# Narrow gate products, state-row spreading and weight splits reordered in a two-layer hybrid decoder step

## The chip, the cores and the metric

One core of a Trainium2 chip runs the whole program. The metric is the device time of one execution in microseconds (us); the median of several runs counts. The engines are TensorE (PE, matrix products), VectorE (DVE, "vector"), ScalarE (ACT), GpSimd (POOL) and SyncE (SP), which issues most loads. Each has its own instruction stream; they wait for one another on semaphores.

## The reference

A prompt of 512 tokens and 8 sample tokens (520 columns in all) go through two layers with shared weights. Layer 0 has gated DeltaNet heads and SSD heads behind one input projection, an output projection `w_out`, and a SwiGLU FFN; layer 1 has latent attention and a second FFN. What the change touches, cut down:

```python
proj = rms_norm(x, norm_g) @ w_in
g_qkv, g_z, g_a, g_b, s_z, s_xbc, s_dt = split(proj)
beta = sigmoid(g_b);  g = -exp(A_log) * softplus(g_a + dt_bias)
dt = softplus(s_dt + ssm_dt_bias)
# recurrences in chunks; at the end of a chunk (for a sample: of its one token)
S = S * exp(last) + einsum('bhjd,bhjv->bhdv', k * exp(last - cum), v_new)
h = h * exp(last) + einsum('bjhn,bjhp->bhpn', B * exp(last - cum), xdt)
x = x + concat([o, y]) @ w_out
x = x + (silu(gate) * up) @ w_down       # gate, up = rms_norm(x) @ w_gate_up
```

The 16 gate columns are g_a (4), s_dt (8) and g_b (4). For the samples each of the 8 sequences has its own states: S of 4 heads x 128 x 128, h of 128 x 512, 2 MB each for all eight. They are decayed, updated by an outer product of a key column and a value row, and stored.

## The kernel before

Activations lie with features on the 128 partitions and 520 tokens in the free dimension, in two halves of 260. Every large weight tile of 128 output features x 1024 is loaded by SP into one of four slots `wring`, rounded to a high half on ACT (`high`, L1191) and completed by a low half on DVE (`low`, L1635). `piece` (L553) then makes 48 products per tile: high weight by high and by low activation, low weight by high activation, over 8 slices of 128 and two halves. A tile goes to bank pair 0/1 or 2/3 of PSUM, alternately, and `gemm_ready` and `tile_taken` hand it over and back. PE's queue runs the stages in the order of `STAGES` (L50): `proj` (7 turns of 4 tiles), the chunked recurrences, `outa` (8 tiles), `gu0` (44), `dn0`, and then layer 1 with `inc`, `uq`, attention, `outc`, `gu1`, `dn1`.

**The gates.** After turn 0 of `proj` PE waits for the scaled gate weights (`gprep_ready`) and for the norm's root, and makes 5 x 8 float32 products in L612 to L617: 128 tokens of `xres` as the stationary operand, `wgate` with 16 columns as the moving one; five more products turn the root into a column. DVE finishes the convolution of turn 0 (`conv_turn`, L1710), then computes softplus and sigmoid from bank 6 (L1735 to L1766), with exponentials from ACT (L1294 to L1298), then goes into the loop of turns 1 to 4 (L1768). A step of that loop evicts a tile (L1720), splits a weight (`low`) and convolves it (L1725 to L1730). ACT applies SiLU and splits weights in the same order (L1272).

**The end of layer 0's mixer.** After the chunks the sample states wait for their update. POOL loads h0, issues the stores of the prompt's states (`rec_stored`), decays s0 and h0 one sequence after the other (L492 to L495), issues two stores of convolution rows and only then adds squares for the next norm (`sum_squares(1)`, L498). PE turns the value rows into rows 0 to 7 (L848 to L855), and ACT copies them to `vrow` and `xrow` (L1411 to L1414). During `outa`, after tile k, `spread_rows(k)` (L857) makes two float32 products per sequence b that copy row b to all 128 partitions, in banks 6 and 7:

```python
mm(PS[:, 6, :], ident[0:8, b:b + 1].broadcast_to([8, 128]), vrow[0:8, :])
```

DVE's `update(b)` (L1988) multiplies bank 6 by the key column (L1992), adds that to s0 once it is decayed (L1995), and does the same for h0 from bank 7 (L1999, L2002). `UPDATES` (L57) puts sequences 6 and 7 behind tile 6. PE waits for update b - 1 before it spreads row b. In `residual` (L1607) DVE waits for `rec_stored`, and then, for each tile k, adds it to `xres`, splits the low half of weight k + 2, makes the low half of the normed activation k - 1 (`gained_low`, L1601), and calls the updates. ACT's `ffn` (L1198) has the same steps: high half of weight k + 2, high half of the activation, its square (L1174), which from the third on waits until POOL has added the one before last. At k = 7 ACT waits for all updates, issues the stores of s0 and h0 (L1208, L1210), and splits the first two weights of `gu0`; their low halves are DVE's, before it takes tile 7. The split weights lie where `vrow`, `xrow` and the update's scratch `supd` lay. After `gu0`'s first tile PE sums the squares over the partitions (`norm_sum`, L599, banks 4 and 5), and ACT makes the root. ACT and DVE then wait until both state stores have landed, since the FFN's activations lie over the states.

## Time and profile before

| | |
|---|---|
| median of 3 runs | 1562.09 us (1559.18 to 1562.7) |
| the profiled execution, its own time | 1566.82 us |
| its span | 1565.1 us |
| mean granted clock of TensorE | 0.971 |
| busy: PE, DVE, ACT, POOL | 96%, 48%, 38%, 10% |

A busy PE is not a PE at its peak: the granted clock says which of its two levels it ran at (1.0 is 2.4 GHz, 0.5 is 1.2 GHz). Idle time of another engine costs nothing as long as PE has work. In the rows below, times are microseconds from the start of the span; a row of a timeline has start, duration, engine, line, operation, output and inputs, and a count where rows are merged; in brackets stands how long the engine was idle before it and what released it. The products have the line of the helper `mm`, L543, so they are told apart by their tiles. `arena` is the large buffer that holds most tensors, s0, h0, `hid`, `mix`, `vrow` and `supd` among them.

### The profile page before, as it was taken

How to read it: one execution, taken by the hardware profiler on the slowest of the kernel's cores; microseconds unless marked ns; L12 is line 12 of the kernel's file. 1: busy time of each engine (PE TensorE's matmuls, PEld its weight loads, DVE VectorE, ACT ScalarE, POOL GpSimd, SP SyncE). 2: the span in 40 equal slices, each digit the busy share in tenths (PEclk: the TensorE clock that was granted, in tenths of full speed). 3: DMA queues.
4: the chain of work that ended last, by engine and by line, in shares of the span. 5: the costliest groups of instructions: out<-in, count | busy, mean ns of one | idle time of the engine just before them, and what ended most of it. 6: DMA issues, size and time to landing. Idle time of an engine off the chain costs nothing.

```text
span 1565.1 us, 29154 instructions
## 1 busy us (share of the span) xinstructions
PE 1504.4 (96%) x11822; PEld 1400.9 (90%) x11822; DVE 753.3 (48%) x1277; ACT 593.6 (38%) x905; POOL 161.0 (10%) x194
## 2 busy tenths in 40 slices
PE   7999988889899999999999999999899999999999
PEld 7999988878779999999999967655699999999998
DVE  7578465677654444443233327355434444443222
ACT  5344532334224434432222364366434344342111
POOL 1000022211710000000010000352020000000000
PEclk9799999999979999999999999699899999999999
DMA  6123100003342233223322421364422322322322
GB/s 220 55 80 94 60 23 28 28 28 132 105 162 82 94 94 94 85 90 103 99 85 88 120 76 36 105 175 152 135 82 82 94 94 83 93 92 88 97 88 78
DMA packets 47983, 144.58 MB, mean 92 GB/s; under 512 B 6848, under 2 KB 16160, under 8 KB 46752
## 3 DMA queue, kind: packets, MB, share of 16 engines
q1 hardware_dynamic: 41472, 118.57, 24.6%
q0 software_dynamic: 6144, 20.73, 4.4%
q10 hardware_dynamic: 288, 4.19, 0.7%
q8 instruction: 53, 0.87, 0.2%
q14 instruction: 26, 0.21, 0.0%
HBM read 134.66 MB, written 7.76 MB: 91 GB/s over the span
## 4 chain that ended last, share of the span: by engine, by line
PE 85%; DVE 6%; issue 4%; ACT 2%; POOL 2%; DMA 1%; DVEq 0%; ACTq 0%; POOLq 0%
PE PS L543 83%; DVE arena L1730 1%; PE PS L1038 1%; POOL arena L494 1%; DMA arena<-in_s_ssm 1%; POOL arena L493 1%; DVE arena L1876 1%; ACT wsplit L1196 0%; DVE arena L1725 0%; DVE arena L1720 0%; DVE arena L1918 0%; DVE wsplit L1641 0%; ACT arena L1539 0%; DMA gains<-in_gains 0%; DVE arena L1899 0%
## 5 line engine op out<-in xcount | busy, mean ns | idle before, releaser
L543 PE MATMUL PS<-xnh,wsplit 128*128 128x260 f32 x3904 | 637.8, 285 | 14.1 <-DVE wsplit L1641 11.5
L543 PEld LDWEIGHTS PS<-xnh,wsplit 128*128 128x128 f32 x3904 | 541.4, 190 | 15.7 <-DVE wsplit L1641 11.9
L543 PE MATMUL PS<-xnl,wsplit 128*128 128x260 f32 x1952 | 394.8, 284 | 0.0
L1196 ACT ACTIVATE wsplit<-wring 128x1024 fp32r<-128x1024 f32 x176 | 182.8, 1040 | 450.9 <-PE PS L543 444.0
L1641 DVE TENSOR_TENSOR wsplit<-wring,wsplit 128x1024 fp32r<-128x1024 f32 x176 | 210.9, 1200 | 215.2 <-ACT wsplit L1196 215.1
L543 PEld LDWEIGHTS PS<-xnl,wsplit 128*128 128x128 f32 x1952 | 302.4, 190 | 0.0
L543 PE MATMUL PS<-hidh,wsplit 128*128 128x260 f32 x1408 | 226.6, 283 | 0.0
L543 PEld LDWEIGHTS PS<-hidh,wsplit 128*128 128x128 f32 x1408 | 192.9, 188 | 0.0
L543 PE MATMUL PS<-arena 128*128 128x128 f32 (+9 forms) x1104 | 179.1, 332 | 13.5 <-DVE arena L1876 7.7
L543 PEld LDWEIGHTS PS<-arena 128*128 128x128 f32 (+2 forms) x1104 | 140.2, 198 | 51.4 <-issue 33.6
L543 PE MATMUL PS<-hidl,wsplit 128*128 128x260 f32 x704 | 141.2, 282 | 0.0
L543 PEld LDWEIGHTS PS<-hidl,wsplit 128*128 128x128 f32 x704 | 108.7, 188 | 0.0
L1655 DVE TENSOR_TENSOR sq<-PS,rinv 128x520 f32<-128x520 f32 x44 | 30.8, 699 | 119.9 <-PE PS L543 119.9
L1660 DVE TENSOR_TENSOR sgate<-PS,rinv 128x520 f32<-128x520 f32 x44 | 30.8, 699 | 119.4 <-PE PS L543 105.7
L1196 ACT ACT_TABLE_LOAD x24 | 30.8, 1283 | 70.4 <-PE PS L543 70.3
L473 POOL TENSOR_TENSOR arena<-arena,cst 128x512 f32<-128x512 f32 x28 | 36.4, 1333 | 160.0 <-DVE arena L1888 160.0
L460 POOL TENSOR_TENSOR sqsum<-sqsum,sq 128x520 f32<-128x520 f32 x18 | 31.8, 1769 | 129.2 <-ACT sq L1179 128.8
L1730 DVE SCALAR_TENSOR_TENSOR arena<-arena,convw 128x512 f32<-128x512 f32 x60 | 44.8, 746 | 0.0
L1379 ACT ACTIVATE arena<-PS 128x256 f32<-128x256 f32 x48 | 18.4, 384 | 61.1 <-PE PS L543 60.0
L1539 ACT ACTIVATE arena<-PS,nb,rqs 128x512 f32<-128x512 f32 (+1 forms) x64 | 38.8, 627 | 5.2 <-DVE nb L2135 5.2
L1235 ACT ACTIVATE hidh<-sgate 128x520 f32 (+1 forms) x44 | 28.2, 640 | 24.8 <-DVE sgate L1658 24.8
L543 PE MATMUL PS<-cqh,wsplit 128*128 128x260 f32 x192 | 37.3, 297 | 0.0
(390 smaller groups left out, 1693.5 us busy)
## 6 DMA issues: line engine op xcount, KB each, us to landing
wring<-in_w_gu SPq DMA_DIRECT2D x88, 512.0 KB, 3.6
wring<-in_w_dn SPq DMA_DIRECT2D x32, 512.0 KB, 3.5
wring<-in_w_proj SPq DMA_DIRECT2D x28, 512.0 KB, 3.6
wring<-in_w_dn SPq DMA_DIRECT2D x16, 384.0 KB, 3.1
wring<-in_w_outa SPq DMA_DIRECT2D x8, 512.0 KB, 3.6
wring<-in_w_inc SPq DMA_DIRECT2D x8, 512.0 KB, 3.6
wring<-in_w_uq SPq DMA_DIRECT2D x8, 512.0 KB, 4.8
wring<-in_w_outc SPq DMA_DIRECT2D x8, 512.0 KB, 4.4
```

The lines of the kernel that those rows point to most:

```text
L460: pool.tensor_tensor(sqsum[:, :], sqsum[:, :], sq[:, k % 2, :], ALU.add).then_inc(s('sq_added'), 1)
L473: pool.tensor_tensor(by(mt[:, l], GH), by(lt, GH), across(const(f'inv{l}'), GH), ALU.mult)\
L493: pool.tensor_tensor(s0[:, :, b], s0[:, :, b], over(ab[:, 0:GH, b], 128), ALU.mult).then_inc(s('s_decayed'), 1)
L543: return pe.matmul(out, lhsT, rhs, start=start, stop=stop)
L1196: act.activation(dst[:, 0:w], wring[u][:, 0:w], ACT.Copy).then_inc(s('w_hi'), 1)
L1235: act.activation(hq, sgate[:, q, :], ACT.Copy).then_inc(s('hid_hi'), 1)
L1379: act.activation(yinv[:, hs_], PS[:, by_, hs_], ACT.Copy).then_inc(s('y_ready'), 1)
L1539: ins = act.activation(pm[:, to:to + w], PS[:, b0 + e, at_:at_ + w], ACT.Exp, bias=nb[:, q:q + 1], scale=rqs[:, q, h:h + 1], accum_out=den ...
L1641: tt(wl[:, 0:w], wring[u][:, 0:w], wh[:, 0:w].bitcast(F32), ALU.subtract).then_inc(s('w_split'), 1)
L1655: tt(two(supt), bank2(2), two(root), ALU.mult).then_inc(tile_taken[1], 1)
L1660: tt(two(sgate[:, q, :]), bank2(0), two(root), ALU.mult).then_inc(tile_taken[0], 1)
L1730: st(stt(out=cacc[:, p, 0:T], in0=raw[:, p, t:t + T], scalar=w(t), in1=cacc[:, p, 0:T], op0=ALU.mult, op1=ALU.add), s('conv_done') if t == ...
```

## The change

**Gates.** The gate weights are padded from 16 to 32 columns. After tile 1 of turn 0 PE makes 16 float32 products in which `wgate` is the stationary operand and `xres` the moving one (260 columns); slice k goes to column group k % 4, so two slices add up in each group of 32 PSUM rows, in banks 4 and 5. ACT copies the result to `gsum` in the third step of turn 0. DVE builds `gsel` from four pieces of the identity. After turn 0, five products of `gsum` with `gsel` add the four groups and turn tokens onto the partitions, beside the five root products that there were.

**Rows.** `vrow` and `xrow` become 64 rows, cleared by ACT during the last chunk; rows 0 to 7 hold the rounded values and rows 32 to 39 what the rounding left, which DVE subtracts. A spreading product is now one of rounded operands (float32r) over 64 rows, with the selector `idr` that the key scale uses later. Sequence b uses banks 4 and 5 or 6 and 7, alternately, and PE waits for update b - 2. One update goes behind each tile.

**Order.** POOL adds squares 0, 1 and 2 between the decays, the rest after them, and issues the convolution stores last. `supd`, `vrow` and `xrow` move away from where `gu0`'s split weights lie; those are split in steps 6 and 7 of `residual`, before the updates of these steps (in layer 1 too). The waits for `rec_stored` and for the state stores move into the FFN, the latter to its fourth turn; ACT issues the state stores after the root.

```diff
-UPDATES = [(0,), (1,), (2,), (3,), (4,), (5,), (6, 7), ()]
+SELECT = (4, 6)
...
+        gsum, gsel = sq[:, 0, :], sq[:, 1, 0:32]
...
-        wgate = sb("wgate", 128, KD, NGATE)
+        wgate = sb("wgate", 128, KD, 32)
...
-        vrow, xrow, supd = take(512), take(512), take(2, 512)
+        supd = hid[:, TK:TK + 2, 0:512]
+        vrow, xrow = (nc.alloc_sbuf_tensor_at(n, [64, 512], F32R, offset=base + 4 * (2 * KD + TK + e) * TOK)
+                      for n, e in (("vrow", 2), ("xrow", 3)))
...
+            def add_square(n, k):
+                pool.wait_ge(s('sq_ready'), KD * n + k + 1)
+                if k == 0:
+                    pool.wait_ge(s('ssq_mm'), n)
+                    pool.tensor_copy(sqsum[:, :], sq[:, 0, :]).then_inc(s('sq_added'), 1)
+                else:
                     pool.wait_ge(s('sq_added'), (KD - 1) * n + k)
                     pool.tensor_tensor(sqsum[:, :], sqsum[:, :], sq[:, k % 2, :], ALU.add).then_inc(s('sq_added'), 1)
...
                 pool.tensor_tensor(by(h0[:, b], SH), by(h0[:, b], SH), over(ab[:, GH:, b], 64), ALU.mult)\
                     .then_inc(s('s_decayed'), 1)
+                if b >= 2 and b % 2 == 0:
+                    add_square(1, b // 2 - 1)
+            sum_squares(1, 3)
             pool.dma_start(O['conv_s'][:, :, 2], convout_s[:, :, :]).then_inc(s('out_stored'), 16)
             pool.dma_start(O['conv_s'][:, :, 0:2], prev[:, :, 1:3]).then_inc(s('out_stored'), 16)
-            sum_squares(1)
...
             def norm_sum(n):
                 if n == 0:
                     pe.wait_ge(c_loaded, 16)
+                if n == 1:
+                    pe.wait_ge(s('sel_taken'), NS - 1)
+                    pe.wait_ge(s('hsel_taken'), NS - 1)
...
-            split_gemm('proj', xnh, xnl, 0, 1, norm=0)
-
-            pe.wait_ge(s('gprep_ready'), 1)
-            pe.wait_ge(s('rinv_ready'), 1)
+            def gate_sums(i, u):
+
+                if u != 1:
+                    return
+                pe.wait_ge(s('gprep_ready'), 1)
+                pe.wait_ge(s('rinv_ready'), 1)
+                for half in range(2):
+                    for k in range(KD):
+                        g = k % 4
+                        ins = mm(PS[32 * g:32 * g + 32, 4 + half, 0:HALF], wgate[:, k, :],
+                                 xres[:, k, half * HALF:(half + 1) * HALF], k < 4, k >= 4)
+                ins.then_inc(s('gates_mm'), 1)
+            split_gemm('proj', xnh, xnl, 0, 1, norm=0, after=gate_sums)
+
+            pe.wait_ge(s('gact_ready'), 1)
+            pe.wait_ge(s('gprep_ready'), 2)
             for t in range(5):
-                for k in range(KD):
-                    toks = slice(t * 128, min((t + 1) * 128, TOK))
-                    mm(PS[0:toks.stop - toks.start, 6, t * NGATE:(t + 1) * NGATE], xres[:, k, toks], wgate[:, k, :],
-                       k == 0, k == KD - 1)
+                toks = slice(t * 128, min((t + 1) * 128, TOK))
+                mm(PS[0:toks.stop - toks.start, 6, t * NGATE:(t + 1) * NGATE], gsum[:, toks], gsel[:, 0:NGATE])
                 ins = mm(PS[0:toks.stop - toks.start, 6, 5 * NGATE + t:5 * NGATE + t + 1], sqsum[:, toks], ident[:, 0:1])
...
-                for b in UPDATES[k]:
...
+                b, bank = k, SELECT[k % 2]
+                one = idr[0:64, b:b + 1].broadcast_to([64, 128])
+                if b == 0:
+                    pe.wait_ge(s('s_ready'), NCH)
+                    pe.wait_ge(s('row_split'), 2)
+                if b >= 2:
+                    pe.wait_ge(s('sel_taken'), b - 1)
+                mm(PS[:, bank, :], one, vrow[:, :]).then_inc(s('sel_mm'), 1)
+                if b >= 2:
+                    pe.wait_ge(s('hsel_taken'), b - 1)
+                mm(PS[:, bank + 1, :], one, xrow[:, :]).then_inc(s('hsel_mm'), 1)
...
-                    if k == KD - 1:
-                        if l == 0:
-                            act.wait_ge(s('sel_taken'), NS)
-                            act.dma_start(O['s_gdn'], s0).then_inc(s('big_stored'), 16)
-                            act.wait_ge(s('hsel_taken'), NS)
-                            act.dma_start(O['s_ssm'], h0).then_inc(s('big_stored'), 16)
+                    if k == KD - 2:
                         for u in range(2):
                             high(gu, 0, u)
...
                 norm_root(n)
-                act.wait_ge(*((s('big_stored'), 32) if l == 0 else (s('out_stored'), 96)))
+                if l == 0:
+                    act.wait_ge(s('sel_taken'), NS)
+                    act.dma_start(O['s_gdn'], s0).then_inc(s('big_stored'), 16)
+                    act.wait_ge(s('hsel_taken'), NS)
+                    act.dma_start(O['s_ssm'], h0).then_inc(s('big_stored'), 16)
+                else:
+                    act.wait_ge(s('out_stored'), 96)
...
+                    if first and u == 2:
+                        act.wait_ge(s('gates_mm'), 1)
+                        act.activation(two(gsum), bank2(4), ACT.Copy).then_inc(s('gact_ready'), 1)
                 silu(3)
             conv_turn(0, True)
+            for e in range(2):
+                act.activation(idr[32 * e:32 * e + 32, :], ident[0:32, 0:16], ACT.Copy)
...
+                    if c == NCH - 1 and l in (2, 4):
+                        act.activation((vrow if l == 2 else xrow)[:, :], cst[0:64, 0:4, :].rearrange("p a t -> p (a t)"), ACT.Copy, scale=0.0)
...
-                if l == 0:
-                    dve.wait_ge(s('rec_stored'), 32)
                 for k in range(KD):
                     p = k % 2
                     if k == KD - 1:
-                        for u in range(2):
-                            low(f'gu{l}', 0, u)
+                        low(f'gu{l}', 0, 1)
...
+                    if k == KD - 2:
+                        low(f'gu{l}', 0, 0)
+                    if after and k < KD - 1:
                         after(k)
                 gained_low(n, KD - 1)
+                if after:
+                    after(KD - 1)
...
-                dve.wait_ge(*((s('big_stored'), 32) if l == 0 else (s('out_stored'), 96)))
+                dve.wait_ge(*((s('rec_stored'), 32) if l == 0 else (s('out_stored'), 96)))
...
+                if l == 0:
+                    with dve.Fori(0, 3) as i:
+                        turn(i)
+                    dve.wait_ge(s('big_stored'), 32)
+                with dve.Fori(0 if l else 3, TURNS[gu] - 1) as i:
...
+            dve.wait_ge(s('ssq_mm'), 1)
+            st(tt(gsel, ident[:, 0:32], ident[:, 32:64], ALU.add))
+            for g in (2, 3):
+                st.sync()
+                st(tt(gsel, gsel, ident[:, 32 * g:32 * g + 32], ALU.add), s('gprep_ready') if g == 3 else None)
...
+            for e, (row, bank) in enumerate(((vrow, 6), (xrow, 4))):
+                dve.wait_ge(s('row_ready'), e + 1)
+                st(tt(row[32:40, :], PS[0:8, bank, :], row[0:8, :].bitcast(F32), ALU.subtract), s('row_split'))
```

## Rows read from the trace of the kernel before

**Rows 1.** Stretches: length, busy PE, PEld, DVE, ACT, POOL, then PE clock, DMA, GB/s.
```profile
37.90:51.60 13.70, 13.70 (x92) 13.67 (x90) 5.00 (x9) 4.09 (x7) 0.00 (x0) 0.59 0.15 42
386.50:462.50 76.00, 70.83 (x415) 56.73 (x416) 48.67 (x58) 19.35 (x26) 37.72 (x29) 0.89 0.41 131
```
**Rows 2.** Timeline of PE: first eight gate products.
```profile
37.92 1.85 PE L543 MATMUL PS<-wgate,xres 128*128 128x16 f32 x16
```
**Rows 3.** Timeline of PE: first of eight such 32-column products, and what follows.
```profile
951.30 0.41 PE L543 MATMUL PS<-sq,qsel 128*32 128x260 f32 x2 [0.90 <-issue]
...
952.31 1.14 PE L543 MATMUL PS<-sqsum,rotg 128*128 128x260 f32 x4
```
**Rows 4.** Timeline of DVE: end of turn 0, the gates, starts of later turns.
```profile
42.87 0.75 DVE L1730 SCALAR_TENSOR_TENSOR arena<-arena,convw 128x512 f32<-128x512 f32 x1
...
51.77 0.12 DVE L1736 MEMSET graw<- 128x80 f32 x1 [8.15 <-PE PS L543]
...
55.70 0.22 DVE L1766 SCALAR_TENSOR_TENSOR la<-gsp,nega 128x60 f32<-128x60 f32 x1
60.20 0.70 DVE L1720 TENSOR_TENSOR arena<-PS,sqsum 128x520 f32<-128x520 f32 x1 [4.28 <-PE PS L543]
62.66 1.22 DVE L1641 TENSOR_TENSOR wsplit<-wring,wsplit 128x1024 fp32r<-128x1024 f32 x1 [1.76 <-ACT wsplit L1196]
...
83.52 0.69 DVE L1720 TENSOR_TENSOR arena<-PS,sqsum 128x520 f32<-128x520 f32 x1
...
131.96 0.69 DVE L1720 TENSOR_TENSOR arena<-PS,sqsum 128x520 f32<-128x520 f32 x1
```
**Rows 5.** Timeline of PE: its longest wait in the loop of turns 1 to 4.
```profile
136.63 0.51 PE L543 MATMUL PS<-xnh,wsplit 128*128 128x260 f32 x2 [0.89 <-DVE wsplit L1641]
```
**Rows 6.** Timeline of PE: outa's start, two spreading pairs, gu0's start, norm sum.
```profile
386.67 0.48 PE L543 MATMUL PS<-mixh,outhi 128*128 128x260 f32 x2 [1.14 <-DVE mixl L1632]
...
439.75 1.98 PE L543 MATMUL PS<-arena,cst 8*128 8x512 f32 x4
...
447.62 1.98 PE L543 MATMUL PS<-arena,cst 8*128 8x512 f32 x4
...
462.69 0.40 PE L543 MATMUL PS<-xnh,wsplit 128*128 128x260 f32 x2
...
468.46 1.04 PE L543 MATMUL PS<-sqsum,cst 128*128 128x260 f32 x4
```
**Rows 7.** Timeline of PE: a key-scale product between two product pairs of a tile.
```profile
956.65 0.40 PE L543 MATMUL PS<-cqh,wsplit 128*128 128x260 f32 x2
956.98 0.46 PE L543 MATMUL PS<-invs,idr 64*96 64x512 f32 x1
...
957.72 0.40 PE L543 MATMUL PS<-cql,wsplit 128*128 128x260 f32 x2
```
**Rows 8.** Timeline of ACT in outa: the third square.
```profile
421.55 0.64 ACT L1179 ACTIVATE sq<-xres 128x520 f32<-128x520 f32 x1 [10.20 <-POOL sqsum L456]
```
**Rows 9.** Timeline of DVE in outa: three residual adds, each the start of a step.
```profile
397.29 0.70 DVE L1619 TENSOR_TENSOR xres<-xres,PS 128x520 f32<-128x520 f32 x1 [6.50 <-DMA out_p_ssm<-arena]
...
402.42 0.68 DVE L1619 TENSOR_TENSOR xres<-xres,PS 128x520 f32<-128x520 f32 x1
...
409.67 0.70 DVE L1619 TENSOR_TENSOR xres<-xres,PS 128x520 f32<-128x520 f32 x1 [0.79 <-PE PS L543]
```
**Rows 10.** Groups by line in outa: busy us, mean ns, idle before.
```profile
L494 POOL TENSOR_TENSOR arena<-arena,spare 128x512 f32<-128x512 f32 x8 | 12.3, 1539 | 0.0
L493 POOL TENSOR_TENSOR arena<-arena,spare 128x512 f32<-128x512 f32 x8 | 11.2, 1395 | 7.2 <-DMA arena<-in_s_ssm 7.2
```
**Rows 11.** Timeline of all engines at gu0's start: state store, split weight, third tile.
```profile
454.04 0.39 ACTq L1208 DMA_DIRECT2D out_s_gdn<-arena  x1
...
474.18 1.23 DVE L1641 TENSOR_TENSOR wsplit<-wring,wsplit 128x1024 fp32r<-128x1024 f32 x1 [1.49 <-ACT wsplit L1196]
...
475.73 0.53 PE L543 MATMUL PS<-xnh,wsplit 128*128 128x260 f32 x3
```

More of the change, by code:

```diff
@@ L451, in _, with sum_squares @@
                 pool.dma_start(dst[:], A[src]).then_inc(g_loaded, 16)
-            def sum_squares(n):
-                pool.wait_ge(s('ssq_mm'), n)
-                pool.wait_ge(s('sq_ready'), KD * n + 1)
-                pool.tensor_copy(sqsum[:, :], sq[:, 0, :]).then_inc(s('sq_added'), 1)
-                for k in range(1, KD - 1):
-                    pool.wait_ge(s('sq_ready'), KD * n + k + 1)
+            def add_square(n, k):
[4 more added lines that the diff above has]
+                else:
                     pool.wait_ge(s('sq_added'), (KD - 1) * n + k)
                     pool.tensor_tensor(sqsum[:, :], sqsum[:, :], sq[:, k % 2, :], ALU.add).then_inc(s('sq_added'), 1)
+            def sum_squares(n, first=0):
+                for k in range(first, KD - 1):
+                    add_square(n, k)
             pool.memset(raw[:, 0, 0:3], 0.0)
@@ L1421, in _ @@
             act.activation(wkrh[:, :, :], wkr, ACT.Copy).then_inc(s('rest_hi'), 1)
-            for e in range(2):
-                act.activation(idr[32 * e:32 * e + 32, :], ident[0:32, 0:16], ACT.Copy)
             act.activation(invs[:, :], cst[0:64, 0:4, :].rearrange("p a t -> p (a t)"), ACT.Copy, scale=0.0)
@@ L1623, in residual @@
                         gained_low(n, k - 1)
-                    if after:
+                    if k == KD - 2:
+                        low(f'gu{l}', 0, 0)
+                    if after and k < KD - 1:
                         after(k)
                 gained_low(n, KD - 1)
+                if after:
+                    after(KD - 1)
             def mix_low(n, *parts):
@@ L1670, in turn @@
                             tt(hl, sgate[:, q, :], hh.bitcast(F32), ALU.subtract).then_inc(s('hid_ready'), 1)
-                with dve.Fori(0, TURNS[gu] - 1) as i:
+                if l == 0:
[3 more added lines that the diff above has]
+                with dve.Fori(0 if l else 3, TURNS[gu] - 1) as i:
                     turn(i)
@@ L1706, in _ @@
             dve.wait_ge(g_loaded, 16 * len(SMALLS))
-            st(tt(wgate[:, :, :], wgate[:, :, :], over(gains[:, 0, :], NGATE), ALU.mult), s('gprep_ready'))
+            st(tt(wgate[:, :, :], wgate[:, :, :], over(gains[:, 0, :], 32), ALU.mult), s('gprep_ready'))
+            dve.wait_ge(s('ssq_mm'), 1)
[3 more added lines that the diff above has]
+                st(tt(gsel, gsel, ident[:, 32 * g:32 * g + 32], ALU.add), s('gprep_ready') if g == 3 else None)
             dve.wait_ge(s('rinv_ready'), 1)
@@ L1733, in _ @@
             conv_turn(0, True)
-            dve.wait_ge(s('gates_mm'), 1)
+            dve.wait_ge(s('gates_mm'), 2)
             st(dve.memset(graw[:, :, :], 0.0))
@@ L1758, in _ @@
             st(tt(gabs[:, :, dc], gabs[:, :, dc], grec[:, :, dc], ALU.mult))
-            dve.wait_ge(s('gact_ready'), 3)
+            dve.wait_ge(s('gact_ready'), 4)
             st.sync()
@@ L1986, in _ @@
             low('outa', 0, 1)
+            for e, (row, bank) in enumerate(((vrow, 6), (xrow, 4))):
+                dve.wait_ge(s('row_ready'), e + 1)
+                st(tt(row[32:40, :], PS[0:8, bank, :], row[0:8, :].bitcast(F32), ALU.subtract), s('row_split'))
             def update(b):
+                bank = SELECT[b % 2]
                 dve.wait_ge(s('sel_mm'), b + 1)
@@ L1991, in update @@
                     dve.wait_ge(s('sel_taken'), b)
-                st(tt(by(supd[:, 0], GH), by(PS[:, 6, :], GH), over(hid[:, TK:TK + 4, T + b], 128), ALU.mult))
+                st(tt(by(supd[:, 0], GH), by(PS[:, bank, :], GH), over(hid[:, TK:TK + 4, T + b], 128), ALU.mult))
                 st.sync()
@@ L1998, in update @@
                     dve.wait_ge(s('hsel_taken'), b)
-                st(tt(by(supd[:, 1], 2), by(PS[:, 7, :], 2), over(hid[:, TB:TB + 2, T + b], 256), ALU.mult))
+                st(tt(by(supd[:, 1], 2), by(PS[:, bank + 1, :], 2), over(hid[:, TB:TB + 2, T + b], 256), ALU.mult))
                 st.sync()
@@ L2002, in update @@
                 st(tt(h0[:, b], h0[:, b], supd[:, 1], ALU.add), s('hsel_taken'))
-            residual('outa', 0, lambda k: [update(b) for b in UPDATES[k]])
+            residual('outa', 0, update)
             ffn(0, 1)
@@ L2312 @@
     f['w_proj'] = _tiles(np.concatenate([qkv, xbc, gz, sz], axis=1))
-    f['w_gate'] = np.ascontiguousarray(np.concatenate([ga, dt, gb], axis=1).reshape(KD, 128, NGATE).transpose(1, 0, 2))
+    f['w_gate'] = np.zeros((128, KD, 32), np.float32)
+    f['w_gate'][:, :, 0:NGATE] = np.concatenate([ga, dt, gb], axis=1).reshape(KD, 128, NGATE).transpose(1, 0, 2)
     f['w_outa'], f['w_outc'] = _tiles(I['w_out_a'][0]), _tiles(I['w_out_c'][0])
```

19 lines of the change are left out of this document (6 added, 13 removed).

## The prediction

> **What bounds the kernel now.** I read the page's busy shares first: TensorE (PE) is busy in nearly every slice, so only places where it idles, runs at a low clock or does work that could go are worth anything. Then the chain of waits, which leaves PE in two places that the change touches; then the table of stretches for both, and each engine's timeline there.
>
> The first place is the gate block after turn 0 of the input projection. It takes 13.7 us at a mean granted clock of 0.59 [rows 1]: 40 float32 products that stream only 16 columns each. Eight of them took 1.85 us before the clock fell, 0.23 each [rows 2]. The reader should see that the clock falls during the block from 2.4 towards 1.2 GHz, and that the next tile pays too: vector's first eviction after it is at 60.20, 8.6 us after 51.6 [rows 4], where a tile at full clock is 5.77 (462.69 to 468.46, [rows 6]).
>
> The second is the output projection `outa`, 386.67 to 462.69, 76.0 us [rows 6]. A tile with one pair of row-spreading products repeats in 7.87 us where nothing waits (439.75 to 447.62), so the pair costs 2.10 beside a tile of 5.77 [rows 6]. Eight are 63.0; the other 13.0 are idle time (5.2, the stretch less PE's busy time) and the lower clock after it (mean 0.89) [rows 1]. The cause shows on ScalarE: a square waited 10.2 us for GpSimd to add an earlier one, behind all decays, and everything queued on ScalarE (the next weight split) came late [rows 8].
>
> **The change part by part.** Gates, added: 16 float32 products of 260 columns into four groups of 32 columns, between tiles 1 and 2 of turn 0. Eight products of exactly that shape took 1.01 us (951.30 to 952.31, [rows 3]), so 2.0. Unoverlapped, a pair takes 1.04 [rows 6], so 8.3 is the upper end; and it could hardly be less, so 2.0 is the lower. I take 2.0: same shape.
> The Trainium skill, page "TensorE: Matmul & The Clock Gate", section "Measured speedup vs the span model", has a speedup of 2.38 for three column groups; an estimate by it would be 8.3 / 2.38 = 3.5 and the forecast 1.5 later, but the trace's rows have four groups at 4.1 times, so I keep them.
> Left after turn 0: ten products, eight with full 128-column weights, 0.23 each [rows 2], about 2.2; at half clock about 4.4. Their inputs (ScalarE's copy, vector's four small adds) are made while tiles 2 and 3 run, 11.5 us, and cost nothing; without that cover PE waits for a copy, some 0.7 like vector's eviction [rows 4]. PE then reaches turn 1 after 4.2 instead of 13.7 us and without the slow tile (2.6): 12.1 earlier.
>
> But the loop that follows is paced by vector. Two of its turns took 48.4 us, from 83.52 to 131.96, 24.2 a turn [rows 4], against 4 x 5.77 = 23.1 for PE, and near its end PE waits 0.89 for vector's split [rows 5]. So vector's start counts. Turn 0's convolution ends at 43.6 now (42.87 plus 0.75) and at 45.6 with the sums ahead of tiles 2 and 3. The gate arithmetic takes 4.15 (51.77 to 55.92); it ran while ScalarE was idle, and now its exponentials wait for ScalarE's last silu, two small copies and a table load, which I put at 1.2 more (between nothing and the 1.76 that such a load made vector wait in turn 1). So turn 1 starts at 45.6 + 4.15 + 1.2 = 50.95 instead of 60.20: 9.25. That wait of 1.76 goes too, as ScalarE splits while vector still calculates. Gates: **-11.0** [rows 4], with bounds of -3 (sums unoverlapped and a slow clock after them) and -12.5.
>
> Spreading: a pair becomes two single-pass products over 64 rows. The nearest rows are the key-scale products of that form: with one inserted, two product pairs of 0.24 (5.77 / 24) and it take 1.07 (956.65 to 957.72, [rows 7]), so 0.59 alone. Two together lie between 2 x 0.24 streamed and 2 x 0.59; I take 0.9, since the switching is paid once. Eight save 8 x 1.2 = 9.6.
>
> Stalls: squares added between decays free ScalarE's queue. Decays take 8 x (1.54 + 1.40) = 23.5 us [rows 10]; with three adds among them, each about as long as a decay, GpSimd is done some 28 us after h0 lands, and each add comes before the square that waits for it. Two bank pairs let PE spread a row while vector uses the one before. Vector's step of add, split, low half and update took 6.46 with GpSimd busy throughout (402.42 to 409.67 less 0.79 idle, [rows 9]); PE's will be 5.77 + 0.9 = 6.67. So vector keeps pace, just, with a lead of about 4 us before PE needs its split. Splitting gu0's first two weights in steps 6 and 7 lets PE go straight on; its last inputs come, by the same steps, about 3 us before they are read, and update 7 then runs under gu0's first tile. Without the wait for the small state stores vector starts at 392.5 (386.67 plus a tile), not 397.29 [rows 9], and its two subtractions for the rounded halves fall into that hole of 6.5. The zeroing of the rows stands between two levels of the last chunk, where ScalarE waits for PE. Nothing for either; about 1.2, two copies, if not covered. outa: 8 x 6.67 = 53.4 instead of 76.0, **-22.6**; bounds -15 (vector bound) and -25.
>
> Moved and added behind it: the two 2 MB stores are now issued by ScalarE after the norm's root, ahead of the split of gu0's third tile. That split landed at 475.41, PE wanted it at 475.7; an issue is 0.39, so two make PE wait **+0.5** [rows 11]. Vector's new wait for the stores stands at turn 3 of gu0, more than 60 us on; nothing; if the weight loads held the stores up that long, the loads would be late themselves. The convolution store goes behind the adds on GpSimd's queue, whose next work waits for the FFN: nothing. In layer 1 the same reorder moves a split that already ended as the tile arrived: nothing.
>
> **Sum.** -11.0 - 22.6 + 0.5 = -33.1. The profiled execution took 1566.82 (span 1565.1) and would take 1533.7; it lies 4.7 above the median of the runs, 1562.09, so I forecast 1529 for the median.
>
> **The rivals.** (1) *The stall stays*: squares, decays and updates still wait for each other, only elsewhere, and PE loses the same 13.0. Then 1529 + 13 = 1542. For it: GpSimd works without a break through most of outa. Against: each add now precedes its square by several us. 10%.
>
> (2) *Vector becomes outa's bound by contention.* Four instructions of a step read two SBUF tensors while GpSimd works; if two of them each stood behind a GpSimd instruction of 1.47 [rows 10] over what rows 9 hold, a step would be 9.4, four steps 2.7 longer each, less the lead of 4, plus about 4 for the clock falling: 1540. Against: the step of 6.46 was already measured under full GpSimd load [rows 9]. 8%.
> The Trainium skill, page "SBUF — State Buffer", section "SBUF: two separate sides", speaks for this: VectorE and GpSimd lock a port pair for a whole instruction and the loser blocks. Taken literally, four blocked instructions add 5.9 to a step; the trace's 6.46 does not hold that.
>
> (3) *The gate sums don't overlap* or PE's clock falls in their tail: 8.3 instead of 2.0 plus some 2 us of half clock, so the gates give 3: 1537. For it: the block of now fell to 0.59 with narrow products. Against: rows 3. 8%.
>
> (4) *Slower*: PE runs outa at 1.2 GHz because its new 64-row products and waits let the clock fall after each tile. Tiles would take up to 11.5 and pairs 1.8, 107 instead of 76, +31, less the gates' 11: 1582. It decides once outa takes over 86.5 us, an average clock below about 0.62. For it: both falls of now follow a wait beside such products. Against: the spacing of 7.87 over a pair [rows 6] and that of the key-scale products [rows 7] are those of the full clock. 3%.
>
> **How the numbers follow.** My forecast has 68%, the rest (3%) is something unforeseen that takes most of the gain. Low end: both best bounds, 1562 - 12.5 - 25 = 1524.5, and 1 for the run's scatter; high end 1541, which takes in rivals 2 and 3 and nearly 1. A measurement here tells some 0.2% (3 us) from nothing. Faster 0.95, same 0.02, slower 0.03.
>
> **What would show it.** The gate block after turn 0 near 2 us at a clock near 1; vector's turn 1 starting near 51; outa near 53 us with no square waiting longer than 1 us and clock 1.0; gu0's third tile waiting about half a us. If outa takes over 60 with PE waiting for `outlo` it is rival 2, for the updates rival 1. A total above 1541 means that a wait I costed at nothing is real.

## The result, and the profile after

The changed kernel takes 1525.24 us (median of 4 runs, 1524.4 to 1530.07) against 1561.47 for the kernel before (4 runs); the ratio is 0.9776, 95% interval 0.9752 to 0.98. It is 36.2 us faster; 33.1 were forecast. Its profiled execution took 1524.4 us (span 1522.7, mean granted clock 0.988).

Where the time went is read at four marks that both traces have: VectorE's first eviction of turn 2, the first product of `outa`, the first of `gu0`, the end.

| stretch | before | after | less |
|---|---|---|---|
| start to turn 2 (gates) | 83.52 | 72.25 | 11.27 |
| turn 2 to `outa` (little touched) | 303.15 | 301.14 | 2.01 |
| `outa` | 76.02 | 52.88 | 23.14 |
| `gu0` to the end | 1102.4 | 1096.4 | 6.0 |

The second and fourth stretches add up to 8.0. Little in them was edited, and the profiled execution of before was 5.35 above its median. Three stretches of each kernel in time order show what differs there (columns: stretch, length, busy us and count of PE, PEld, DVE, ACT, POOL, granted clock, DMA share, GB/s). Before, the second chunk stretch and layer 1's attention with what follows it:

```profile
240.00:270.00 30.00, 25.86 (x195) 24.70 (x193) 17.46 (x43) 8.73 (x16) 9.11 (x7) 0.89 0.05 22
...
950.00:1130.00 180.00, 165.69 (x1244) 111.51 (x1242) 97.03 (x258) 97.56 (x231) 51.98 (x97) 0.91 0.43 130
1130.00:1200.00 70.00, 69.30 (x553) 69.06 (x554) 27.86 (x34) 26.69 (x35) 11.29 (x7) 0.96 0.25 76
```

And the changed kernel, the same stretches:

```profile
228.70:258.70 30.00, 25.17 (x214) 23.74 (x213) 18.29 (x45) 8.48 (x16) 9.09 (x7) 0.94 0.01 1
...
913.60:1092.00 178.40, 163.78 (x1275) 110.44 (x1274) 99.20 (x262) 97.60 (x231) 51.81 (x97) 0.94 0.42 131
1092.00:1159.00 67.00, 67.00 (x554) 66.77 (x553) 28.77 (x32) 26.55 (x34) 11.59 (x7) 1.00 0.27 79
```

About the same work (the counts differ by a few records) ran at a granted clock of 0.94 instead of 0.89, and of 0.94 and 1.00 instead of 0.91 and 0.96. In the traces of this study the stretch from turn 2 to `outa` takes 300.9 to 304.5 us where nothing in it was edited, and the one from `gu0` to the end 1094.7 to 1106.0. Runs of one kernel, too, lie up to 13 us apart below. So each edit is judged by its own stretch first and by its median second.

The touched stretches of the changed kernel, in the table by stretch: the gate sums, what is left after turn 0, and `outa`.

```profile
26.00:28.10 2.10, 2.10 (x35) 1.06 (x34) 2.06 (x5) 1.29 (x3) 0.00 (x0) 1.00 0.41 166
39.60:41.70 2.10, 2.10 (x23) 2.06 (x22) 1.50 (x2) 1.87 (x4) 0.00 (x0) 1.00 0.01 4
373.40:426.30 52.90, 52.90 (x401) 48.93 (x401) 49.27 (x56) 19.39 (x26) 38.86 (x28) 1.00 0.42 132
```

These answer to [rows 1]: the block of 13.7 us at 0.59 is 2.1 us at 1.00, and `outa` at 0.89 with idle time is 52.9 at 1.00 without any. The timeline of TensorE and VectorE at the places in question:

```profile
26.07 1.97 PE L552 MATMUL PS<-xres,wgate 128*32 128x260 f32 x32
...
48.20 0.20 DVE L1790 TENSOR_SCALAR gone<-gexp 128x80 f32<-128x80 f32 x1 [1.56 <-ACT gexp L1327]
...
50.73 0.70 DVE L1761 TENSOR_TENSOR arena<-PS,sqsum 128x520 f32<-128x520 f32 x1 [0.17 <-issue]
51.39 1.23 DVE L1673 TENSOR_TENSOR wsplit<-wring,wsplit 128x1024 fp32r<-128x1024 f32 x1
...
72.25 0.69 DVE L1761 TENSOR_TENSOR arena<-PS,sqsum 128x520 f32<-128x520 f32 x1
...
379.32 0.49 PE L552 MATMUL PS<-vrow,idr 64*128 64x512 f32 x1
379.65 0.39 PE L552 MATMUL PS<-xrow,idr 64*128 64x512 f32 x1
385.93 0.49 PE L552 MATMUL PS<-vrow,idr 64*128 64x512 f32 x1
...
440.00 0.48 PE L552 MATMUL PS<-xnh,wsplit 128*128 128x260 f32 x2 [0.18 <-DVE wsplit L1673]
```

The sums take 1.97 us. VectorE's turn 1 starts at 50.73, where [rows 4] have 60.20, and its split at 51.39 waits for nothing, where it waited 1.76. A tile with its pair repeats in 6.61 us (379.32 to 385.93), so the pair costs 0.84 beside the 5.77 of [rows 6]. The third tile of `gu0` waits 0.18 for its split. No square on ScalarE waits for GpSimd any more, where [rows 8] show 10.20.

### The profile page after: what moved, and what is told of

It is laid out like the page before. It is cut to its first block, busy times and chain, and to the rows that moved or that the text cites. A ratio compares the mean times of both kernels' runs of the same rounds, so it can differ in the third digit from the quotient of the medians.

```text
span 1522.7 us, 29056 instructions
## 1 busy us (share of the span) xinstructions
PE 1465.8 (96%) x11768; PEld 1371.3 (90%) x11768; DVE 757.4 (50%) x1282; ACT 594.5 (39%) x908; POOL 162.3 (11%) x194
## 4 chain that ended last, share of the span: by engine, by line
PE 86%; DVE 7%; issue 4%; ACT 3%; DVEq 0%; DMA 0%; ACTq 0%; POOLq 0%
PE PS L552 84%; DVE arena L1771 2%; PE PS L1063 1%; DVE arena L1917 1%; ACT wsplit L1221 0%; DVE arena L1761 0%; DVE arena L1766 0%; DVE wsplit L1673 0%; DVE arena L1959 0%; ACT arena L1570 0%; DMA gains<-in_gains 0%; DVE arena L1940 0%; DVE arena L1769 0%; ACT arena L1392 0%; ACT arena L1559 0%
## 5 line engine op out<-in xcount | busy, mean ns | idle before, releaser
L552 PE MATMUL PS<-arena 128*128 128x128 f32 (+9 forms) x1104 | 171.5, 323 | 13.1 <-DVE arena L1917 7.7
L552 PEld LDWEIGHTS PS<-arena 128*128 128x128 f32 (+2 forms) x1104 | 134.2, 191 | 50.1 <-issue 31.7
```

The lines of the kernel that those rows point to most:

```text
L552: return pe.matmul(out, lhsT, rhs, start=start, stop=stop)
```

## The experiments

Twelve more measurements follow, one of them of the changed kernel itself. Below, "the stage" is `outa` from its first product to `gu0`'s first: 76.02 before, 52.88 in the changed kernel. The last column gives the ratio to the kernel before, measured beside it, with its interval.

| kernel | stage, us | median (range), us | ratio (interval) |
|---|---|---|---|
| changed, once more | 52.85 | 1525.1 (1524.31 to 1527.33) | 0.9762 (0.9742 to 0.9781) |
| narrow gates | 52.85 | 1534.75 (1532.99 to 1537.93) | 0.9827 (0.9806 to 0.9848) |
| one column group | 52.91 | 1532.1 (1531.44 to 1541.96) | 0.9808 (0.9789 to 0.9827) |
| adds last | 54.58 | 1525.58 (1524.73 to 1528.06) | 0.9773 (0.9753 to 0.9794) |
| one bank pair | 55.15 | 1534.62 (1531.51 to 1537.32) | 0.9832 (0.9812 to 0.9852) |
| adds last, one pair | 61.31 | 1532.64 (1532.3 to 1540.77) | 0.9825 (0.9794 to 0.9856) |
| the same, and store wait | 64.83 | 1536.43 (1535.09 to 1537.25) | 0.9829 (0.9807 to 0.9852) |
| float32 rows | 62.93 | 1539.69 (1535.46 to 1546.74) | 0.9857 (0.9831 to 0.9884) |
| before, adds between | 67.07 | 1556.15 (1547.98 to 1561.07) | 0.9959 (0.9938 to 0.9979) |
| split late | 52.88 | 1530.24 (1525.16 to 1536.82) | 0.9808 (0.978 to 0.9836) |
| no decays | 52.85 | 1531.32 (1525.18 to 1536.12) | 0.9798 (0.977 to 0.9825) |
| SiLU later | 52.85 | 1522.29 (1521.16 to 1522.47) | 0.9739 (0.9721 to 0.9758) |

**The changed kernel once more.**

> The changed kernel once more, unedited, beside the three that follow. Four runs of it lay at 1524.4 to 1530.1; kernels that differ from it where TensorE has slack lay between 1525 and 1537 on another chip, at a mean granted clock of 0.987 or of 0.980. Theory: that spread is the chip's, so this kernel shows it too on some chips, median 1525 to 1531. Rival: the spread belongs to those edits, and this one stays within 1524 to 1527.

It stayed between 1524.31 and 1527.33, which speaks for the rival. With the first measurement that is nine runs between 1524.3 and 1530.1, at mean granted clocks of 0.983 to 0.988; see the late split below for what stays open.

**Narrow gates.** The old gate block, the rest changed:

```diff
-            split_gemm('proj', xnh, xnl, 0, 1, norm=0, after=gate_sums)
+            split_gemm('proj', xnh, xnl, 0, 1, norm=0)
...
-                mm(PS[0:toks.stop - toks.start, 6, t * NGATE:(t + 1) * NGATE], gsum[:, toks], gsel[:, 0:NGATE])
+                for k in range(KD):
+                    mm(PS[0:toks.stop - toks.start, 6, t * NGATE:(t + 1) * NGATE], xres[:, k, toks], wgate[:, k, 0:NGATE],
+                       k == 0, k == KD - 1)
...
```

> The changed kernel with the old gate block: 40 narrow products after turn 0, no products in column groups, the rest of the change kept. My theory: the loop of turns 1 to 4 is paced by VectorE, so what the gates give is VectorE's earlier start in turn 1, 11.3 us in the trace of the changed kernel (turn 2 at 72.25 instead of 83.52): median 1525.2 + 11.3 = 1536.5 (1535 to 1538), and the block again near 13.7 us at a granted clock near 0.6. Rival A: what counts is TensorE's own path there, 12 to 16 us: 1538 to 1541. Rival B: the gate part gives little and the spreading brought nearly all of it: 1526 to 1531.

The median is 9.5 us above the changed kernel, just under the theory's 1535 to 1538 and in neither rival's range. Turn 2 starts at 80.21, 7.96 later than with column groups, and the timeline of the block says why that is less than 11.3:

```profile
37.73 1.85 PE L552 MATMUL PS<-wgate,xres 128*128 128x16 f32 x16
...
39.65 1.94 PE L552 MATMUL PS<-wgate,xres 128*128 128x16 f32 x16
...
41.66 3.06 PE L552 MATMUL PS<-wgate,xres 128*128 128x16 f32 x16
...
44.99 3.57 PE L552 MATMUL PS<-wgate,xres 128*128 128x16 f32 x16
...
80.21 0.69 DVE L1756 TENSOR_TENSOR arena<-PS,sqsum 128x520 f32<-128x520 f32 x1
```

The kernel before, the second eight of the same products:

```profile
39.85 3.20 PE L543 MATMUL PS<-wgate,xres 128*128 128x16 f32 x16
```

Eight took 1.85 [rows 2] as long as the clock held. Here it held for sixteen and fell among the third eight; in the trace of before it fell among the second. The block took 11.7 us instead of 13.7. A third trace with the old block, that of the kernel before with the adds between (below), has its turn 2 at 81.63, 9.4 later than the changed kernel:

```profile
81.63 0.69 DVE L1726 TENSOR_TENSOR arena<-PS,sqsum 128x520 f32<-128x520 f32 x1
```

So the gate part is worth between 8 and 11.3 us, by when the clock falls in the old block.

**One column group.** All slices add up in the same 32 rows:

```diff
-                        g = k % 4
-                        ins = mm(PS[32 * g:32 * g + 32, 4 + half, 0:HALF], wgate[:, k, :],
-                                 xres[:, k, half * HALF:(half + 1) * HALF], k < 4, k >= 4)
+                        ins = mm(PS[0:32, 4 + half, 0:HALF], wgate[:, k, :],
+                                 xres[:, k, half * HALF:(half + 1) * HALF], k == 0, k == KD - 1)
...
-                mm(PS[0:toks.stop - toks.start, 6, t * NGATE:(t + 1) * NGATE], gsum[:, toks], gsel[:, 0:NGATE])
+                mm(PS[0:toks.stop - toks.start, 6, t * NGATE:(t + 1) * NGATE], gsum[0:32, toks], gsel[0:32, 0:NGATE])
```

> The changed kernel with all 16 gate products in one group of 32 columns, each slice adding to the same rows of the bank; five products over 32 rows follow instead of 128. Theory: without neighbours in other column groups they run one after the other, 16 x 0.52 = 8.3 us instead of 1.97, TensorE and behind it VectorE are 6.3 later in turn 0 and everything after: 1525.2 + 6.3 = 1531.5 (1529.5 to 1533). Rival A: one group costs nothing, since the overlap comes from pipelining and not from the groups: 1525 to 1526. Rival B: the clock falls during the longer block and the tiles behind it too: 1534 or later.

```profile
26.12 7.20 PE L552 MATMUL PS<-xres,wgate 128*32 128x260 f32 x32
```

The same 16 products take 7.20 us instead of 1.97, at a clock of 1.00, and turn 2 starts 5.29 later (77.54). The overlap comes from the groups (that all slices now also add up in the same rows was not tested apart), and TensorE's loss here (5.23) is VectorE's. The Trainium skill, page "TensorE: Matmul & The Clock Gate", section "Measured speedup vs the span model", gives 2.38 for three groups; four measured 7.20 / 1.97 = 3.65 here.

**Adds last.** All squares added behind the decays:

```diff
-                if b >= 2 and b % 2 == 0:
-                    add_square(1, b // 2 - 1)
-            sum_squares(1, 3)
+            sum_squares(1)
```

> The changed kernel with all adds of squares behind the decays again; the convolution stores stay behind the adds. The prediction put the whole stall of 13.0 us on this order: then 1525.2 + 10 to 13 = 1535 to 1538. Rival, worked out from the rows of the changed kernel: the decays would end near 405.6, square 2 would wait some 11 us, and the split of the sixth output weight would land near 409 instead of 402; TensorE wants it at 406.6, so it waits only 2 to 4 us: 1527 to 1529; the other 9 to 11 us then came from VectorE's late start, the stores ahead of the adds and the single pair of banks.

The stage is 1.7 us longer, so the theory falls. The rival has the mechanism right and too high a price: TensorE waits 1.65, not 2 to 4, and the median is only 0.3 above the changed kernel's. In the timeline ScalarE's square waits as long as in [rows 8], and TensorE waits once:

```profile
405.30 0.64 ACT L1202 ACTIVATE sq<-xres 128x520 f32<-128x520 f32 x1 [9.63 <-POOL sqsum L460]
...
409.34 0.48 PE L550 MATMUL PS<-mixh,outhi 128*128 128x260 f32 x2 [1.65 <-DVE outlo L1671]
```

**One bank pair.**

```diff
-SELECT = (4, 6)
+SELECT = (6, 6)
...
-                if b >= 2:
-                    pe.wait_ge(s('sel_taken'), b - 1)
+                if b:
+                    pe.wait_ge(s('sel_taken'), b)
```

(and so for `hsel_taken`).

> The changed kernel with banks 6 and 7 alone for the spread rows; TensorE waits for update b - 1 again. Theory: VectorE's step (6.65 us) is hardly longer than TensorE's period (6.61), so each spreading waits for what VectorE lags, 0 to 1.5 us, and the period becomes VectorE's: +0 to +3, 1525 to 1528. Rival: with one pair, the tile, the spreading and the update stand one behind the other (6.6 plus an update of 2.8 less what fits beside it), a period of 7.5 or more: +7 and more, 1532 or later.

The stage is 2.3 us longer, as the theory had it. The timeline shows two waits of the second product of a pair for VectorE's update before:

```profile
395.08 0.50 PE L552 MATMUL PS<-xrow,idr 64*128 64x512 f32 x1 [0.70 <-DVE arena L2047]
...
409.40 0.49 PE L552 MATMUL PS<-xrow,idr 64*128 64x512 f32 x1 [0.77 <-DVE arena L2047]
```

The median lies 9.4 higher, as the rival had it. The profiled run, 1531.51, has 1.3 more ahead of the stage and 3.5 behind it, in code that wasn't edited; the other runs have no trace. All five runs lie between 1531.5 and 1537.3, at mean granted clocks of 0.980 to 0.984 (the changed kernel: 1524.3 to 1530.1, 0.983 to 0.988), so it is not one odd execution. Where the rest of the 9.4 comes from stays open.

**Both, and both with the wait for the state stores.** First the two edits above together; then also

```diff
+                if l == 0:
+                    dve.wait_ge(s('rec_stored'), 32)
                 for k in range(KD):
```

in `residual`, with the convolution stores ahead of the adds.

> The changed kernel with the adds behind the decays and with one pair of banks. Alone, the first made the output projection 54.6 us instead of 52.9, the second 55.2. Theory: the two delays feed each other, as in the kernel before: VectorE, held by ScalarE's late split, updates late, TensorE cannot spread the next row, idles and its clock falls: 60 us or more, time 1532 to 1540. Rival: they add up: 56.5 to 57.5 us, 1528 to 1532.

> As the kernel with adds last and one pair of banks, and also VectorE's wait for the prompt's state stores ahead of the first tile and the convolution stores ahead of the adds: the order of the kernel before, with the new products, one update for each tile and the early split of gu0. Theory: the whole stall of before comes back, the output projection takes 52.9 + 13 = 66 us (63 to 67), time 1536 to 1541. Rival: the shorter products leave room for a good part of it: 58 to 62 us, 1530 to 1535.

Both theories hold: 8.4 us for the pair of edits, twice the 4.0 of the two alone, and 11.95 with the wait and the place of the convolution stores. In the first kernel's timeline VectorE's split waits for ScalarE's half of the weight, which stands behind the square, and TensorE then stands for 4.88 us:

```profile
407.25 2.27 DVE L1671 TENSOR_TENSOR outlo<-wring,outhi 128x1024 fp32r<-128x1024 f32 x1 [5.41 <-ACT outhi L1219]
...
412.60 0.79 PE L550 MATMUL PS<-vrow,idr 64*128 64x512 f32 x1 [4.88 <-DVE arena L2038]
```

In the second kernel's timeline VectorE starts late (4.52), and in the middle TensorE stands for 5.60 us; its next products take 0.79 where 0.49 was seen before:

```profile
385.96 0.70 DVE L1647 TENSOR_TENSOR xres<-xres,PS 128x520 f32<-128x520 f32 x1 [4.52 <-DMA out_p_ssm<-arena]
...
410.68 0.64 ACT L1202 ACTIVATE sq<-xres 128x520 f32<-128x520 f32 x1 [10.21 <-POOL sqsum L460]
...
417.65 0.79 PE L550 MATMUL PS<-vrow,idr 64*128 64x512 f32 x1 [5.60 <-DVE arena L2040]
418.98 0.79 PE L550 MATMUL PS<-xrow,idr 64*128 64x512 f32 x1 [0.54 <-DVE arena L2047]
```

Its rows in the table by stretch have 57.03 busy of 64.83 us at a clock of 0.92, and a clock of 0.50 right after the wait:

```profile
376.00:440.83 64.83, 57.03 (x400) 52.13 (x401) 46.90 (x56) 19.15 (x26) 37.33 (x28) 0.92 0.38 110
...
417.60:420.00 2.40, 1.81 (x3) 0.87 (x4) 2.37 (x4) 0.44 (x1) 0.00 (x0) 0.50 0.01 2
```

**Float32 rows.** Products over 8 rows as before, `vrow` and `xrow` in float32:

```diff
-                one = idr[0:64, b:b + 1].broadcast_to([64, 128])
+                one = ident[0:8, b:b + 1].broadcast_to([8, 128])
...
-                mm(PS[:, bank, :], one, vrow[:, :]).then_inc(s('sel_mm'), 1)
+                mm(PS[:, bank, :], one, vrow[0:8, :]).then_inc(s('sel_mm'), 1)
```

(and so for `xrow`).

> The changed kernel with float32 products of 8 rows for the spreading (the form of before), rows in float32, the two pairs of banks kept. Theory: a pair takes 2.10 us as before instead of 0.84, and TensorE has no idle time in the output projection that could hide it: 8 x 1.26 = 10.1, 1535.3 (1534 to 1537). Rival: VectorE paces this stage (step 6.65), so only what exceeds its step shows, and the longer period gives VectorE its lag back: the sum is a little under, 8 x (7.87 - 6.65) = 9.8, or much less (1528) if the cost was one of the stall and not of the products.

The stage is 62.93, 10.05 longer, at a clock of 1.00 without idle time: the theory's 10.1. A tile and its pair take 7.87 again (382.13 to 390.00):

```profile
382.13 1.12 PE L552 MATMUL PS<-vrow,cst 8*128 8x512 f32 x2
383.09 1.02 PE L552 MATMUL PS<-xrow,cst 8*128 8x512 f32 x2
390.00 1.12 PE L552 MATMUL PS<-vrow,cst 8*128 8x512 f32 x2
```

The runs lie between 1535.5, as expected, and 1546.7, with mean granted clocks from 0.987 to 0.979; the median, 1539.69, is above the theory's 1534 to 1537. The trace is of the slowest run and has 2.8 more ahead of the stage and 9.6 behind it.

**Before, with the adds between the decays.** The edit to GpSimd's queue alone (adds and convolution stores), in the kernel before:

```diff
...
+                if b >= 2 and b % 2 == 0:
+                    add_square(1, b // 2 - 1)
+            sum_squares(1, 3)
             pool.dma_start(O['conv_s'][:, :, 2], convout_s[:, :, :]).then_inc(s('out_stored'), 16)
             pool.dma_start(O['conv_s'][:, :, 0:2], prev[:, :, 1:3]).then_inc(s('out_stored'), 16)
-            sum_squares(1)
```

> The kernel before with one edit alone: squares 0 to 2 added between the decays, the rest after them, the convolution stores last. The prediction's attribution: the stall of 13.0 us comes from this order, so it goes: 1561.5 - 10 to 13 = 1548.5 to 1551.5, and the output projection takes some 63 to 66 us instead of 76. Rival: VectorE's late start behind the state stores, the single pair of banks and the float32 pairs hold most of the stall: a gain of 0 to 6, 1555 to 1562.

```profile
384.78:451.85 67.07, 66.19 (x417) 53.54 (x418) 48.80 (x57) 19.26 (x26) 39.14 (x28) 0.95 0.42 128
```

The stage loses 8.95 of the 13.0 us, a little under the theory's 10 to 13. The median falls by 6.3 us only (1562.49 to 1556.15), the upper end of the rival, over runs 13 us apart.

**Split late.** `gu0`'s first two weights split at step 7, behind update 6:

```diff
-                    if k == KD - 2:
+                    if k == KD - 1:
                         for u in range(2):
                             high(gu, 0, u)
...
-                        low(f'gu{l}', 0, 1)
+                        for u in range(2):
+                            low(f'gu{l}', 0, u)
...
-                    if k == KD - 2:
-                        low(f'gu{l}', 0, 0)
```

> The changed kernel with gu0's (and gu1's) first two weights split at step 7 again, behind update 6, both halves of the work. The prediction counted the early split as needed for TensorE to go straight on. By the rows of the changed kernel the late split of the first weight would land at 426.1 with TensorE there at 426.27, the second near 427.3 with 432 wanted: 0 to +1, 1525 to 1526.5. Rival: ScalarE's part comes after the square of tile 6 and is 2 us or more too late, TensorE waits and the clock falls: +2 to +5, 1527 to 1530.

The stage is 52.88 and `gu0`'s third tile waits the same 0.18: the early split gives nothing once the stall is gone. Three of its runs lie at 1525.2 to 1526.9 (mean granted clock 0.985 to 0.987), three at 1533.6 to 1536.8 (0.979 to 0.981). The changed kernel, measured later on the same chip, shows nothing of the second kind. The only trace is of the fastest, so whether this edit or chance brought the lower clock stays open.

**No decays.**

```diff
-                pool.tensor_tensor(s0[:, :, b], s0[:, :, b], over(ab[:, 0:GH, b], 128), ALU.mult).then_inc(s('s_decayed'), 1)
+                pool.tensor_tensor(s0[:, 0, b, 0:8], s0[:, 0, b, 0:8], over(ab[:, 0:1, b], 8)[:, 0, :], ALU.mult).then_inc(s('s_decayed'), 1)
```

(and so for `h0`).

> The changed kernel without the decays of the sample states: GpSimd multiplies 8 columns of each instead of all, so s0 and h0 come out undecayed; all waits and adds stay. It frees GpSimd and the SBUF ports while VectorE updates. Theory: GpSimd lengthens VectorE's step (about 5.5 us by itself, 6.65 beside the decays), but TensorE's 6.61 sets the period either way: 1525.2, no difference (within 1), and VectorE's instructions back at 0.75 and 1.22. Rival: VectorE's lag behind GpSimd costs TensorE something that the trace hides in the splits: 1 to 3 us faster.

The stage is the same to 0.03 us, as the theory had it. The median is 6.1 us above the changed kernel, over runs that spread like those of the late split; the trace, of 1532.91, has its 8.5 us over the changed kernel ahead of the stage (3.5) and behind it (5.0). VectorE's step without the decays, in the timeline:

```profile
396.13 0.69 DVE L1647 TENSOR_TENSOR xres<-xres,PS 128x520 f32<-128x520 f32 x1 [0.57 <-PE PS L552]
397.22 1.23 DVE L1673 TENSOR_TENSOR outlo<-wring,outhi 128x1024 fp32r<-128x1024 f32 x1 [0.40 <-ACT outhi L1221]
398.36 0.75 DVE L1635 SCALAR_TENSOR_TENSOR xnl<-xres,gains,xnh 128x520 fp32r<-128x520 f32 x1
```

And with them, in the changed kernel:

```profile
400.38 0.68 DVE L1647 TENSOR_TENSOR xres<-xres,PS 128x520 f32<-128x520 f32 x1
400.99 1.48 DVE L1673 TENSOR_TENSOR outlo<-wring,outhi 128x1024 fp32r<-128x1024 f32 x1
402.39 1.54 DVE L1635 SCALAR_TENSOR_TENSOR xnl<-xres,gains,xnh 128x520 fp32r<-128x520 f32 x1
...
407.04 0.68 DVE L1647 TENSOR_TENSOR xres<-xres,PS 128x520 f32<-128x520 f32 x1
```

GpSimd lengthens the split from 1.23 to 1.48 and the low half from 0.75 to 1.54, and uses up the 0.57 and 0.40 that VectorE otherwise waits. The step becomes 6.66 (400.38 to 407.04) where TensorE needs 6.61: VectorE falls behind by little and TensorE sees none of it.

**SiLU later.** A version that follows from the gates' rows: in the changed kernel VectorE still waits 2.70 us per turn of the loop, for a split that ScalarE makes after the turn's last SiLU.

```profile
75.65 1.23 DVE L1673 TENSOR_TENSOR wsplit<-wring,wsplit 128x1024 fp32r<-128x1024 f32 x1 [2.70 <-ACT wsplit L1221]
```

```diff
...
                 take_tile(0)
+                if not first:
+                    silu(-1)
                 for u in range(1, 4):
...
-                silu(3)
             conv_turn(0, True)
-            for e in range(2):
-                act.activation(idr[32 * e:32 * e + 32, :], ident[0:32, 0:16], ACT.Copy)
...
+            conv_silu(4, 3)
+            for e in range(2):
+                act.activation(idr[32 * e:32 * e + 32, :], ident[0:32, 0:16], ACT.Copy)
```

(`conv_silu(i, u)` is the old `silu(u)` of turn i.)

> The changed kernel with the last SiLU of each convolution turn moved behind ScalarE's first weight split of the next turn, and the two copies of the selector moved behind the loop. In the changed kernel VectorE waits 2.70 us in every turn for that split, which stands behind the SiLU and a table load, and 1.56 us for the exponentials of the gates. Theory: both waits go, VectorE's turn falls from 24.2 to some 21.5 and TensorE's 23.1 paces the loop: the last tile of turn 4 is evicted near 134.5 instead of 139.54, 5 us sooner, 1520 (1518.5 to 1522). Rival: the table load stands in front of the split in any order, VectorE waits on, and only the 1.56 goes: 1523 to 1525.

It is 2.8 us faster than the changed kernel measured beside it, with no overlap of the runs, and beats both kernels (1.9 us between the two profiled executions). VectorE's loop ends 4.9 us sooner (134.86 against 139.78), as the theory said; its timeline still has half of the wait:

```profile
73.25 1.23 DVE L1678 TENSOR_TENSOR wsplit<-wring,wsplit 128x1024 fp32r<-128x1024 f32 x1 [1.38 <-ACT wsplit L1221]
...
134.86 0.69 DVE L1766 TENSOR_TENSOR arena<-PS,sqsum 128x520 f32<-128x520 f32 x1
...
146.65 0.70 DVE L1896 TENSOR_TENSOR arena<-PS,sqsum 128x520 f32<-128x520 f32 x1 [1.64 <-PE PS L552]
```

But VectorE then waits for TensorE, and two tiles after the loop its lead over the changed kernel is down to 3.2 (146.65 against 149.86). The changed kernel's second trace shows what there was to gain, TensorE's waits for VectorE in the loop (a third, of 0.50, stands at 77.15); here there is none:

```profile
101.37 0.51 PE L552 MATMUL PS<-xnh,wsplit 128*128 128x260 f32 x2 [0.89 <-DVE wsplit L1673]
...
125.59 0.51 PE L552 MATMUL PS<-xnh,wsplit 128*128 128x260 f32 x2 [0.89 <-DVE wsplit L1673]
```

They sum to 2.28, near the 1.9 and 2.8 that the time fell by. The theory took VectorE's lateness for the gain and was 2 us too high.

## Why the prediction was right

**Gates: right, -11.0 against 11.27.** The sums took 1.97 for 2.0 (and 7.20 in one group, where 8.3 was the upper end), the ten products left over 2.0 for 2.2, VectorE's turn 1 started at 50.73 for 50.95, and the 1.76 went. VectorE waited 1.56 for ScalarE's exponentials; in the kernel before it had waited 0.43, which is within the prediction's 4.15, so ScalarE's lateness cost 1.13 where 1.2 was put:

```profile
53.57 0.20 DVE L1749 TENSOR_SCALAR gone<-gexp 128x80 f32<-128x80 f32 x1 [0.43 <-ACT gexp L1296]
```

That VectorE's start counts was right: in the kernel with one group a delay of 5.23 reaches turn 2 as 5.29. VectorE paces the loop by little, though: TensorE waits 2.28 for it in the whole loop, and with the SiLU later not at all. And the size depends on the old block's clock: against its two other traces the part is worth 8.0 and 9.4, so that it came out within 0.3 is in part luck.

**Spreading products: right, 9.6 against 10.05**, by the float32 kernel; the pair costs 0.84 where 0.9 was taken.

**The stall of 13.0: right in size, wrong in the step that explains it.** The prediction named one cause, squares behind the decays, and gave the second pair of banks and the removed wait for the state stores no price of their own. In the kernel before the one edit removes 8.95. In the changed kernel undoing it costs 1.7, undoing the banks 2.3, both 8.4, and with the store wait and the old place of the convolution stores 11.95. So no single wait made the stall: a square that waits 10 us for GpSimd does so in the kernel with 54.6 as in the one with 64.8. It takes that square and the single pair of banks together: the square holds up VectorE's split, the split holds up the update behind it, and TensorE must have that update before it spreads the next row. Then it stands for about 5 us (4.88, and 5.60 with VectorE's late start), and its clock falls. 11.95 and 10.05 add up to 22.0 of the 23.14; that they may be added, no run shows. The rest, 1.1, has no run to place it: two updates behind one tile and the late split were not undone together with these.

**The early split: no effect** (the late one cost 0.00 in the stage). The prediction let TensorE go straight on because of it; in the stage and at `gu0`'s third tile it goes straight on without it.

**The state stores ahead of the third split: 0.18 against +0.5.**

**Contention (rival 2): real, and off the path.** VectorE's step became 6.66 where 6.46 was used, against 6.61 of TensorE; the margin was thinner than the prediction's, and the lead of 4 us covered it (the split that starts at 400.99 ends 3.95 before its tile starts, at 406.42). The Trainium skill, page "SBUF — State Buffer", section "SBUF: two separate sides", has the loser of the shared ports blocked for a whole instruction of the other; the two instructions above lost 0.25 and 0.79 us, not the 1.47 each that its literal reading gave.

Rivals 1, 3 and 4 fall by the rows of the changed kernel: `outa` has no idle time and a clock of 1.00, and the sums took 1.97.

**The sum.** In the median 36.2 against 33.1, near the low end of the range. The terms account for 1.1 of the difference (11.27 + 23.14 - 0.18 = 34.2); the other 2.0 lies, as far as the traces tell, in stretches that the change hardly touches and whose clock differs between the traces. Why it differs stays open.

## What to carry to other kernels

Where several engines hand a stage on to each other, each extra wait may be cheap and two of them dear (1.7 and 2.3 alone, 8.4 together): price them together, or undo them together. A product that fills a quarter of the columns should share the array with three others (1.97 us against 7.20 here). The row of narrow products cost twice, once in itself (13.7 us) and once by the clock after it (8.6 for the next tile, where 5.77 is usual). Freeing the engine that paces a loop gives what the next one waits for it (2.28), not what it is late (4.9).

## What the hardware showed that was not expected

The granted clock in the chunks and in layer 1's attention differs between traces of code that wasn't edited (0.91 and 0.96 against 0.94 and 1.00 above). Runs of one program differ too: with the late split, three have a mean clock of 0.985 to 0.987 and three of 0.979 to 0.981, up to 11.7 us apart, more than several of these edits. The same narrow products took 1.94 us for eight in one kernel's trace and 3.20 in another's at the same place. And the four column groups gave 3.65 times the speed of one.
